# Third layer of a six-layer model: the projection's last columns cut as 256 and 280, ScalarE evacuating both halves of its chunks, and transposes, scales and rotations issued inside it

## The reference

```python
def _nsa_mixer(h, w_in, q_gain, k_gain, cmp_pos, w_cmp, w_out, cos, sin):
    q, kc, vc, ks, vs, kw, vw, gates = split(h @ w_in)    # widths 1024, 6 x 256, 24: 2584 columns
    q = rope(rms_norm(q, q_gain)); kc, ks, kw = [rope(rms_norm(k, gain_i)) for k in (kc, ks, kw)]
    gates = sigmoid(gates)
    kc = einsum(kc[blocks of 32, stride 16] + cmp_pos[0], w_cmp[0])    # 15 compressed keys
    vc = einsum(vc[blocks of 32, stride 16] + cmp_pos[1], w_cmp[1])    # 15 compressed values
    p_c = masked_softmax(q @ kc);  o_c = p_c @ vc
    o_s = masked_softmax(q @ ks) @ vs
    o_w = masked_softmax(q @ kw) @ vw
    return (g[0] * o_c + g[1] * o_s + g[2] * o_w) @ w_out
```

## Time and profile before

| | before |
|---|---|
| median of 3 runs | 1950.72 us |
| the profiled execution's time | 1953.09 us |
| its span, first to last instruction | 1951.3 us |
| mean granted TensorE clock | 0.987 of full |
| PE, DVE, ACT busy | 1876.3, 1134.9, 923.8 us |

### The profile page before, as it was taken

The page is one execution under the profiler, slowest core; times in us unless marked ns, Lnnn a source line. Parts: engine busy times, 40 slices in busy tenths (PEclk is TensorE's granted clock), DMA queues, the critical chain, the costliest instruction groups (busy, mean ns, idle before and its releaser), DMA issues. The chain is left out here.

```text
span 1951.3 us, 29289 instructions
## 1 busy us (share of the span) xinstructions
PE 1876.3 (96%) x11654; PEld 1638.3 (84%) x11654; DVE 1134.9 (58%) x1643; ACT 923.8 (47%) x1271; POOL 176.5 (9%) x221
## 2 busy tenths in 40 slices
PE   7999999998999999899999999999899999999998
PEld 6668999766899978689998789998679998779997
DVE  6576555767655578554545465446765445775443
ACT  4564343556434446554435455345245435564342
POOL 1400000050000030001000001002501001000000
PEclk9999999999999999799999999999999999999999
DMA  7504555550355555126555425554825454525551
GB/s 249 182 23 131 182 193 186 182 173 17 124 194 193 192 187 176 55 87 216 173 202 185 173 87 176 199 185 164 226 90 173 172 195 151 198 103 173 185 202 66
DMA packets 185357, 313.10 MB, mean 160 GB/s; under 512 B 18877, under 2 KB 67571, under 8 KB 185267
## 3 DMA queue, kind: packets, MB, share of 16 engines
q1 hardware_dynamic: 182595, 304.24, 46.0%
q0 software_dynamic: 1376, 4.38, 0.9%
q10 hardware_dynamic: 1296, 3.24, 0.5%
HBM read 309.90 MB, written 1.94 MB: 160 GB/s over the span
## 5 line engine op out<-in xcount | busy, mean ns | idle before, releaser
L1468 DVE TENSOR_TENSOR w_lo<-raw,w_hi 128x2048 fp32r<-128x2048 f32 (+2 forms) x290 | 654.5, 2287 | 287.6 <-ACT w_hi L998 286.9
L998 ACT ACTIVATE w_hi<-raw 128x2048 fp32r<-128x2048 f32 (+2 forms) x290 | 533.3, 1877 | 105.4 <-PE tr L2039 59.8
L2037 PE MATMUL acc<-w_hi,hT_hi 128*128 128x512 f32 (+2 forms) x688 | 270.0, 392 | 15.5 <-DVE w_lo L1468 8.9
L2039 PE MATMUL acc<-w_hi,hT_lo 128*128 128x512 f32 (+2 forms) x688 | 266.4, 387 | 0.0
L2038 PE MATMUL acc<-w_lo,hT_hi 128*128 128x512 f32 (+2 forms) x688 | 266.2, 387 | 0.0
L2037 PE MATMUL acc<-w_hi,aux_hi 128*128 128x512 f32 x608 | 237.1, 390 | 0.0
L2038 PE MATMUL acc<-w_lo,aux_hi 128*128 128x512 f32 x608 | 237.1, 390 | 0.0
L2039 PE MATMUL acc<-w_hi,aux_lo 128*128 128x512 f32 x608 | 236.5, 389 | 0.0
L2037 PE MATMUL up<-hT_hi,w_hi 128*128 128x256 f32 x768 | 217.7, 283 | 0.6 <-DVE w_lo L1468 0.6
L2037 PE MATMUL tr<-hT_hi,w_hi 128*128 128x256 f32 x768 | 217.3, 283 | 0.0
L2038 PE MATMUL tr<-hT_lo,w_hi 128*128 128x256 f32 x768 | 217.3, 283 | 0.0
(11 more groups left out here) (365 smaller groups left out, 2774.8 us busy)
## 6 DMA issues: line engine op xcount, KB each, us to landing
raw<-in_mlp_w_up SPq DMA_DIRECT2D x64, 1024.0 KB, 6.5
raw<-in_mlp_w_down SPq DMA_DIRECT2D x64, 1024.0 KB, 5.5
raw<-in_ffn_w_gate_up SPq DMA_DIRECT2D x88, 512.0 KB, 4.8
raw<-in_ffn_w_down SPq DMA_DIRECT2D x22, 1024.0 KB, 5.0
raw<-in_w_in SPq DMA_DIRECT2D x16, 1024.0 KB, 8.2
raw<-in_sb_w_in SPq DMA_DIRECT2D x12, 1024.0 KB, 5.2
raw<-in_moba_w_in SPq DMA_DIRECT2D x12, 1024.0 KB, 5.1
raw<-in_nsa_w_in SPq DMA_DIRECT2D x10, 1024.0 KB, 5.7
```

What stands on the lines that cost most here:

```text
L998: nc.scalar.activation(w_hi[:, p0.slot, 0:p0.floats], raw[:, p0.slot, 0:p0.floats], ACT.Copy)\
L1468: nc.vector.tensor_tensor(w_lo[:, p0.slot, 0:m], raw[:, p0.slot, 0:m], f32(w_hi[:, p0.slot, 0:m]), ALU.subtract).then_inc(sem["lo_ready"], 1)
L2037: nc.tensor.matmul(dst, hi, whi, start=first, stop=False)
L2039: return nc.tensor.matmul(dst, lo, whi, start=False, stop=last)
```

## The change

The list of chunks is written out: 1024 to 1535, 0 to 511, 512 to 1023, 1536 to 2047, then 2048 to 2303 (256 columns) and 2304 to 2583 (280 columns). ScalarE evacuates both halves of every chunk of this projection and VectorE none. ScalarE's and VectorE's steps for i = 3 stand before their evacuation of chunk 3 instead of behind it. Steps that stood behind the last chunk stand inside it: two of the four query jobs and the turn of the compressed keys between the last chunk's two pieces on TensorE, and on ScalarE and VectorE the copies, scales and rotations of head set 2 ahead of the chunk's evacuation. The split of the next two pieces, those of `w_out`, stays early on ScalarE, and its `w_lo` moves behind the rotations on VectorE. Three `keep_clock` matmuls are added behind the jobs. The gates are made as an exponential on ScalarE, and an addition and a reciprocal on VectorE, and not as a sigmoid on ScalarE.

```diff
+NSA_CUTS = ((1024, 512), (0, 512), (512, 512), (1536, 512), (2048, 256), (2304, 280))
...
@@ ScalarE, gemm @@
-                    split_next()
+                    if ph.mix is not None and (ph.mix.kind, i) == ("nsa", 5):
+                        nsa_ahead(ph.mix)
+                    else:
+                        split_next()
+                    if ph.mix is not None and (ph.mix.kind, i) == ("nsa", 3):
+                        cmp_raw(ph.mix, 1)
+                        cmp_hi(ph.mix, 0)
+                        heads_scale("nsa", 1)
...
+                    if ph.mix is not None and ph.mix.kind == "nsa":
+                        nc.scalar.activation(proj[:, 1, n0:n0 + w], sum_bank(ph, i, 1)[:, 0:w], ACT.Copy,
+                                             scale=norm_rstd[:, 1:2]).then_inc(sem["evac_d"], 1)
...
-            def nsa_5(ph):
+            def nsa_ahead(ph):
+                cmp_out(ph, 1)
                 cmp_raw(ph, 0)
+                split_next()
+                nsa_job(2, 0)
+                nsa_job(3, 1)
+                cmp_out(ph, 0)
                 heads_scale("nsa", 2)
-                cmp_out(ph, 1)
...
@@ ScalarE, mix_nsa @@
-                for jj in range(2, 6):
+                for jj in range(4, 6):
                     nsa_job(jj, jj - 2)
-                nc.scalar.activation(gates, proj[:, :, 2560:2584], ACT.Sigmoid).then_inc(sem["gate_ready"], 1)
-                cmp_out(ph, 0)
...
                 nsa_job(8, 6)
+                act.wait_ge(sem["evac_d"], n["evac_d"])
+                nc.scalar.activation(gates, proj[:, :, 2560:2584], ACT.Exp, scale=-1.0).then_inc(sem["gate_exp"], 1)
...
@@ VectorE, gemm @@
-                    split_next()
+                    if ph.mix is not None and (ph.mix.kind, i) == ("nsa", 5):
+                        for t in range(TT):
+                            heads_rope("nsa", 2, t)
+                    else:
+                        split_next()
+                    if ph.mix is not None and (ph.mix.kind, i) == ("nsa", 3):
+                        dve.wait_ge(sem["piece_used"], ph.mix.cmp[1][1] + 1)
+                        cmp_lo(0)
+                        heads_rope("nsa", 1, 0)
...
@@ VectorE, mix_nsa @@
+                split_next()
                 dve.wait_ge(sem["prep"], n["prep"] + 6)
...
-                dve.wait_ge(sem["gate_ready"], n["gate_ready"] + 1)
+
+                def gates_close():
+                    dve.wait_ge(sem["gate_exp"], n["gate_exp"] + 1)
+                    link(nc.vector.tensor_scalar(gates, gates, 1.0, None, ALU.add))
+                    link(nc.vector.reciprocal(gates, gates))
...
@@ TensorE, gemm @@
+                        if ph.mix is not None and (ph.mix.kind, i, k0) == ("nsa", 5, 0):
+                            pe.wait_ge(sem["prep"], n["prep"] + 4)
+                            for jj in range(2, 4):
+                                job(jj, jobs_for("nsa")[jj - 2][0], n["pt_evac"])
+                            cmp_turn(0)
...
@@ TensorE, mix_nsa @@
-                pe.wait_ge(sem["prep"], n["prep"] + 4)
-                for jj in range(2, 6):
+                for jj in range(4, 6):
                     job(jj, jobs[jj - 2][0], n["pt_evac"])
-                cmp_turn(0)
+                pe.wait_ge(sem["evac_a"], n["evac_a"] - 1)
+                pe.wait_ge(sem["evac_d"], n["evac_d"] - 1)
+                keep_clock(acc[:, 0, 0:S], 3)
```

More of the change, by code:

```diff
@@ L180, in __init__, with add_gemm @@
         self.variant, self.first, self.n, self.per, self.ups, self.downs, self.kt = variant, first, n, per, ups, downs, kt
-def add_gemm(plan, w, k_rows, width, out, order=None, between=None):
+def add_gemm(plan, w, k_rows, width, out, order=None, between=None, cuts=None):
     chunks = []
     kt_all = k_rows // P
-    for n0 in (range(0, width, W) if order is None else [W * c for c in order]):
-        n = min(W, width - n0)
+    if cuts is None:
+        cuts = [(n0, min(W, width - n0)) for n0 in (range(0, width, W) if order is None else [W * c for c in order])]
+    for n0, n in cuts:
         pieces = []
@@ L278, in add_cmp @@
                                      for half in range(2)]
-                g1 = add_gemm(plan, A["nsa_w_in_2"][0], D, width, "proj", (2, 0, 1, 3, 4, 5),
-                              {2: lambda: add_cmp(1), 4: lambda: add_cmp(0)})
+                g1 = add_gemm(plan, A["nsa_w_in_2"][0], D, width, "proj", None,
+                              {2: lambda: add_cmp(1), 4: lambda: add_cmp(0)}, NSA_CUTS)
                 g1.counts["tab_ready"] = 1
@@ L1205, in _ @@
                        ("nsa", 0): lambda ph: heads_square("nsa", 0), ("nsa", 1): nsa_1, ("nsa", 2): nsa_2,
-                       ("nsa", 3): nsa_3, ("nsa", 4): nsa_4, ("nsa", 5): nsa_5,
+                       ("nsa", 4): nsa_4,
                        ("mixA", 0): A_0, ("mixA", 1): A_1, ("mixA", 2): A_2, ("mixA", 3): A_3}
@@ L1309, in mix_nsa @@
                     0: c_exp, 4: lambda: c_turn_out(0), 5: lambda: c_turn_out(1), 6: lambda: c_turn_out(2),
-                    7: lambda: c_turn_out(3), 14: lambda: mix_out_hi((0, 1), 10),
+                    7: lambda: c_turn_out(3),
+                    14: lambda: mix_out_hi((0, 1), 10),
                     16: lambda: mix_out_hi((2, 3), 12), 18: lambda: mix_out_hi((4, 5), 14)})
@@ L1539, in gemm @@
                         continue
-                    if ph.out == "x":
+                    if ph.mix is not None and ph.mix.kind == "nsa":
+                        pass
+                    elif ph.out == "x":
                         for t in range(TT):
@@ L1805, in cmp_taps @@
                 t0 = (8, 14)[b]
+                if b == 0:
+                    dve.wait_ge(sem["aux_lo"], n["aux_lo"] + 1)
                 dve.wait_ge(sem["pt_evac"], n["pt_evac"] + 2 - b)
@@ L1838, in nsa_4 @@
                 heads_root("nsa", 2)
-            def nsa_5(ph):
-                for t in range(TT):
-                    heads_rope("nsa", 2, t)
             def moba_3(ph):
@@ L1877, in c_norm @@
                         .then_inc(sem["c_prob"], 1)
-                unit_pipeline(units_nsa(), {2: c_norm, 15: lambda: mix_out_lo((0, 1)), 17: lambda: mix_out_lo((2, 3))})
+                unit_pipeline(units_nsa(), {0: gates_close, 2: c_norm, 15: lambda: mix_out_lo((0, 1)), 17: lambda: mix_out_lo((2, 3))})
                 mix_out_lo((4, 5, 6, 7))
```

13 lines of the change are left out of this document (3 added, 10 removed).

## The result

The changed kernel takes 1934.37 us (median of 4 runs, 1932.27 to 1935.03) against 1950.64 us before: 16.3 us less, a ratio of 0.9911 with a 95% interval of 0.9899 to 0.9924. The forecast was 13.4 us less. On two other occasions, beside fresh runs of the kernel before, the same kernel gave 1935.19 against 1949.91 us (0.9925, 0.9912 to 0.9939) and 1934.85 against 1950.47 us (0.9922, 0.9908 to 0.9935), so 14.7 and 15.6 us less.

The account below looks back on a forecast made before the run. TensorE, busy 96% of the span, bounds the kernel; what counts is how much earlier VectorE takes the first unit. 11.85 + 1.8 - 0.2 = 13.4 us, from 1950.7 to 1937.3 us; range 1933.5 to 1942.0.

Parts of the forecast that it names:

- the course of the clock: TensorE's compressed scores: clock falls about 2 us into them, so they take 4.9 us, saving 1.8 of 6.7.
- the clock holds to the units: Rival, chance 0.12: full clock through the compressed scores, `w_lo` bound the first unit at 787.7; 1934.2 to 1935.2 us.
- the likeliest case: The clock falls within the compressed scores; chance 0.51, own range 1935.5 to 1939.5 us.
- TensorE then waits for ScalarE until 780.4: Ahead of the compressed scores: TensorE, its jobs and `keep_clock` products done, idles until ScalarE lets the scores start.
- the sum: 11.85 for the scores' earlier start + 1.8 for the clock - 0.2 for the gates = 13.4 us less.
- Columns: Last two projection chunks at 256 and 280 columns take 11.9 us instead of 17.4: 5.5 us less.
- What stands ahead of the taps' product: ScalarE's scales and splits come 5.8 us earlier; TensorE waits about 0.7 us and starts the product at 763.3.
- To the end of the projection: Taps' product, chunk 5, two jobs and turn: TensorE ends the projection at 776.1, 5.2 us earlier.
- ScalarE's path: ScalarE's queue behind the `w_out` splits lets the compressed scores start at 780.4 against 792.25: 11.85 us earlier.
- VectorE: Rotations end at 782.0, `w_lo` at 786.4, masks at 787.7; first unit at 789.75, so `w_lo` are covered by 2 us.
- The units: The unit stage stays 40 us as before; gates' addition and reciprocal on VectorE cost 0.2 us.
- I assume that all behind it moves with it: Everything behind VectorE's first unit shifts earlier by as much as that unit does.

Follow-up runs that it names:

- e8: The changed kernel with ten `keep_clock` matmuls in the fifth layer's convolution, ahead of TensorE's wait for the fifth stack; 1935.81 us, ratio 0.9923.
- e16: The changed kernel, unaltered, profiled again, against the kernel before; a single execution took 1936.45 us.
- e17: The changed kernel, unaltered, profiled once more, against the kernel before; a single execution took 1937.58 us.

## Why the forecast was off

**The step that failed** is the course of the clock: "I expect the clock to fall about 2 us into them: 2.0 + 14 x 0.209 = 4.9 us". In three of the five profiles of the changed kernel it holds through all 32 scores, which take 3.56 us. That was a rival, "the clock holds to the units", at 0.12 and with 1934.2 to 1935.2 us. Its mechanism is in the rows: `w_lo`, mask and first unit on VectorE without a wait. It put the unit's start at 787.7 - 704.85 = 82.85 from the layer's first product; measured 82.18 to 82.52. But the clock did not hold to the units, it fell 0.1 to 0.5 us ahead of their first products, and the 1 us more that this rival gave to the first units did not come. The medians, 1934.37, 1935.19 and 1934.85, lie in its range; as they mix executions of unknown course, that is partly luck. In the other two profiles, and in e8, the likeliest case came as described, 2.4 us into the scores, and the `w_out` gemm stands at 125.1 to 125.3 against the forecast's 125.4. So the paths in both cases are right. What failed is the choice: one course taken for all executions, with 0.12 for the other, which came in three of five. The reasoning drew on one stretch before, in which 24-column products let the clock fall 4.1 us after they began. It also had TensorE idle ahead of the scores ("TensorE then waits for ScalarE until 780.4", 2 us); that wait is 0.1 us. The missing wait does not by itself explain the held clock, since it is as short in e16 and e17, where the clock fell.

In the first profile the layer gains 15.9 us where the sum had 13.4. Of the 2.5 us between them, 1.3 are the scores' clock (3.13 us saved, not 1.8), 0.9 their earlier start (12.7, not 11.85) and 0.3 the way from the scores to VectorE's first unit (4.09 us against 4.43 before), for which the sum had nothing.

The Trainium skill ("TensorE: Matmul & The Clock Gate", HAM oscillation) has idle gaps as what loses the clock. By it the clock would hold here. Through the scores it does so three times in five, and then falls with no wait of TensorE longer than 0.74 us near; in the other two it fell inside the scores with TensorE busy (4.66 of 4.66 us in e16).

**The other terms.**
- *Columns*: 256 columns start every 0.120 us and 280 every 0.130 (24 in 3.12 us, 768.66 to 771.78), the forecast's 0.119 and 0.130. The 0.119 that the forecast worked out for 280 columns from the Trainium skill ("TensorE: Matmul & The Clock Gate", back-to-back issue gap) is not what the rows show.
- *What stands ahead of the taps' product*: 5.64 us earlier against 5.8, and a wait of 1.24 instead of 0.7, since TensorE was at the turn at 761.44, sooner than I had it.
- *To the end of the projection*: 71.84 against 71.25 for the end; the jobs inside cost 0.97 us (771.78 to 772.75), not 0.7, and the turn 0.17, not 0.1.
- *ScalarE's path*: the scores start 12.5 to 12.9 us earlier, not 11.85, most of the rest by the second piece of `w_out`: on hand 67.5 us behind the layer's first product (771.81), I had 68.25 (773.1). It came 6.8 us behind the `w_lo` that frees its slot (written at 764.97), not 7.7. The scales' roots, which the forecast named as the bound if the pieces landed sooner, end at 774.45, just ahead of the first scale at 774.65; of the five profiles only e16 has the scales wait for them, by 0.1 us.
- *VectorE*: rotations and `w_lo` as forecast; the `w_lo` are covered by 1.25 us (e17), forecast 2, in the course with the fall, and set the start in the other.
- *The units* were to stay at 40.3 and 0.2 for the gates: 40.57 where the clock holds. In the two other profiles a second fall inside them costs 1.1 more, and cancels most of the 1.3 to 1.4 by which their first unit is early. That their `w_out` gemm comes within 0.3 us of the forecast's 125.4 is luck to that extent.
- *"I assume that all behind it moves with it"* holds: the span behind the `w_out` gemm is 1107.6 and 1105.2 us in two profiles of before and 1103.2, 1103.6, 1105.3, 1105.0, 1105.0 in five of the changed kernel; the spread is mostly the clock in the convolution and the wait ahead of it.

Together: 15.9 or 13.7 us from the third layer, by course, against 14.7 to 16.3 in the medians. Elsewhere single executions of one kernel differ by chance, by up to 2.5 us ahead of the layer and 2.4 behind it. Which share of the timed runs had which course is not known, as they have no trace.

## What to carry to other kernels

A gain by narrower work on one engine exists only if what that engine waits for next is brought forward by as much; e1, the new cuts without the new orders, lost 2.4 us. A longer wait can also cost clock in the work behind it, as it did there. Where a stage ends in many narrow products, look at what stands directly ahead of them: give "the clock holds" and "it falls" their own times and comparable chances, and expect both from one kernel. Before a difference between two profiles is put down to a change, take the stage's length in a second execution of each.

## What was not expected of the hardware

- One kernel, two courses of the granted clock in the same 4 us of the program, 2.2 us apart at the stage's end, with the start of the taps' product within 0.04 us and the scores' start within 0.4 us of each other in all five profiles.
- Where the columns are few, a product's price appears to be that of its weights: 15 columns on 128 x 128 weights start every 0.111 us, with the weight load busy for 3.56 of 3.56 us. The taps' product has 128 columns on weights of 128 x 30 and starts every 0.06 us (762.92, 762.98).
